# Differential attention: two banks' low-part score products on 64-row halves of the array, and VectorE's scaling put between the two maxima

## The reference, cut to what matters

```python
s = einsum('bqhmd,bkhmd->bhmqk', q, k) * QK_DIM ** -0.5     # m = 0, 1: two maps for each head
p = softmax(s, axis=-1)
a = p[:, :, 0] - lam * p[:, :, 1]
o = einsum('bhqk,bkhd->bqhd', a, v)
```

## Time and profile before

| what | us |
| --- | --- |
| median of 3 runs (lowest to highest) | 1229.45 (1229.1 to 1230.09) |
| the profiled execution: its time; its span in the trace | 1230.16; 1228.4 |
| TensorE's matmuls busy (share of the span) | 1104.3 (90%) |
| VectorE busy | 608.9 (50%) |
| ScalarE busy | 415.6 (34%) |
| GpSimd busy | 238.0 (19%) |
| attention stage, from its first matmul to the last scaling | 480.9 to 681.9 |

### The profile page before, as it was taken

The page is one execution under the profiler, slowest core; times in us unless marked ns, Lnnn a source line. Parts: engine busy times, 40 slices in busy tenths (PEclk is TensorE's granted clock), DMA queues, the critical chain, the costliest instruction groups (busy, mean ns, idle before and its releaser), DMA issues. The chain is left out here.

```text
span 1228.4 us, 20703 instructions
## 1 busy us (share of the span) xinstructions
PE 1104.3 (90%) x7006; PEld 794.9 (65%) x7006; DVE 608.9 (50%) x1049; ACT 415.6 (34%) x831; POOL 238.0 (19%) x163
## 2 busy tenths in 40 slices
PE   5799999998999997989889799997899869899965
PEld 1687777777999886888788688887533213233332
DVE  0763545204564687767777456666133222233336
ACT  2651111113423774666566546631000000000012
POOL 0000000003000394457666100000111010010041
PEclk9899999999999998899999899998799989999988
DMA  9436677622100544460611333313968873768266
GB/s 362 143 127 235 231 236 237 192 69 79 42 21 1 126 115 132 79 142 24 153 35 52 109 135 106 118 70 134 376 225 279 267 269 124 267 226 264 114 241 255
DMA packets 127944, 196.96 MB, mean 160 GB/s; under 512 B 20592, under 2 KB 93200, under 8 KB 125790
## 3 DMA queue, kind: packets, MB, share of 16 engines
q1 hardware_dynamic: 98700, 144.39, 36.7%
q10 hardware_dynamic: 23378, 30.27, 7.1%
q0 software_dynamic: 5760, 20.97, 5.2%
HBM read 382.85 MB, written 39.24 MB: 344 GB/s over the span
## 5 line engine op out<-in xcount | busy, mean ns | idle before, releaser
L2199 PE MATMUL experts_gu_ps<-moe_wgu,experts_xT 128*32 128x512 f32 x1408 | 169.2, 620 | 18.7 <-DMA moe_wgu<-in_w_exp_up 18.1
L103 PE MATMUL proj_acc_ps<-proj_w_hi,hidden_hT_hi 128*128 128x512 f32 x288 | 117.5, 408 | 6.7 <-DVE hidden_hT_lo L98 6.7
L2199 PEld LDWEIGHTS experts_gu_ps<-moe_wgu,experts_xT 128*32 128x32 f32 x1408 | 43.9, 112 | 121.7 <-issue 101.9
L105 PE MATMUL proj_acc_ps<-proj_w_hi,hidden_hT_lo 128*128 128x512 f32 x288 | 114.8, 399 | 0.0
L104 PE MATMUL proj_acc_ps<-proj_w_lo,hidden_hT_hi 128*128 128x512 f32 x288 | 114.3, 397 | 0.0
L1334 POOL TENSOR_TENSOR att_e<-att_e 128x1152 f32<-128x1152 f32 (+1 forms) x36 | 86.1, 2392 | 71.2 <-DVE att_e L1415 71.2
L1352 ACT ACTIVATE att_e<-att_sc_ps,att_shift 128x1152 f32<-128x1152 f32 (+1 forms) x72 | 81.5, 1132 | 40.2 <-DVE att_shift L1404 39.9
L2220 PE MATMUL experts_y_ps<-moe_wd,experts_hidT 128*32 128x512 f32 x704 | 81.6, 605 | 9.3 <-issue 8.0
L1404 DVE TENSOR_REDUCE att_shift<-att_sc_ps 128x1 f32<-128x1152 f32 (+1 forms) x72 | 86.2, 1231 | 6.7 <-PE att_sc_ps L1449 6.6
L1478 PE MATMUL att_turned_ps<-att_in_v_tok,att_aT 128*128 128x128 f32 x584 | 77.2, 280 | 8.3 <-ACT att_aT L1360 8.1
L2169 POOL DMA_INDIRECT experts_xg<-scratch_h,all_step_token x22 | 30.9, 1406 | 257.0 <-PE experts_x_ps L2184 231.5
(11 more groups left out here) (380 smaller groups left out, 2158.1 us busy)
## 6 DMA issues: line engine op xcount, KB each, us to landing
moe_wgu<-in_w_exp_up ACTq DMA_DIRECT2D x356, 256.0 KB
moe_wgu<-in_w_exp_gate SPq DMA_DIRECT2D x356, 256.0 KB
moe_wd<-in_w_exp_down SPq DMA_DIRECT2D x89, 1024.0 KB
scratch_y_slots<-experts_y ACTq DMA_DIRECT2D x22, 512.0 KB, 5.5
proj_raw<-in_w_in SPq DMA_DIRECT2D x32, 256.0 KB, 5.0
proj_feat<-in_w_ada SPq DMA_DIRECT2D x4, 2048.0 KB, 8.4
proj_xh<-in_w_ada SPq DMA_DIRECT2D x4, 2048.0 KB, 9.9
proj_feat<-in_w_ada SPq DMA_DIRECT2D x4, 1024.0 KB, 8.0
```

What stands on the lines that cost most here:

```text
L103: pe.matmul(out, a_high, b_high, start=start, stop=False)
L105: return pe.matmul(out, a_low, b_high, start=False, stop=stop)
L2199: mm = pe.matmul(gu_ps[n % 2][at, :], xT[:, n % 2, k * P + c * Q:k * P + (c + 1) * Q], wgu[:, c, k], start=(k == 0), stop=(k == KT - 1))
```

## The change

First, the low-part products. `scores` now issues the three high-key matmuls of a map one after another, and then three matmuls that use only 64 of the array's rows: query high times key low, without low times low. Two of them stand on opposite halves of the rows and write different banks, the third is on the first one's half again. For this each half of the rows holds other banks' low keys, and the high part of the query stands on both halves (in a third slab). Second, VectorE's `maximum(k, 0)` moves ahead of `scale_second(k-1)`. Third, `load_stack` issues 18 loads in place of 12.

```diff
+SCORES = TILES * P // 3
+STACK_LOADS = 18
 def load_stack(sp, W, h):
+    keys, queries, done = W["keys"][h % 2], W["queries"][h % 2], W["stack_in"][h % 2]
     for m in range(2):
         rows = slice(m * QKD, (m + 1) * QKD)
-        for part, src in enumerate((W["k_high"], W["k_low"])):
-            for half in range(2):
-                sp.dma_start(W["keys"][h % 2][half * QKD:(half + 1) * QKD, m, part].bitcast(F32), src[h, rows, :]
-                             ).then_inc(W["stack_in"][h % 2], 16)
-        for half, src in enumerate((W["q_high"], W["q_low"])):
-            sp.dma_start(W["queries"][h % 2][half * QKD:(half + 1) * QKD, m].bitcast(F32), src[h, rows, :]
-                         ).then_inc(W["stack_in"][h % 2], 16)
+        own, other = (slice((m ^ half) * QKD, ((m ^ half) + 1) * QKD) for half in range(2))
+        banks = [slice(P + b * SCORES, P + (b + 1) * SCORES) for b in range(3)]
+        for half in (own, other):
+            sp.dma_start(keys[half, m].bitcast(F32), W["k_high"][h, rows, :]).then_inc(done, 16)
+        low = W["k_low"][h, rows, :]
+        for half, to, src in ((own, slice(0, P), slice(0, P)), (own, banks[0], banks[m]), (own, banks[1], banks[2]),
+                              (other, banks[2], banks[1 - m])):
+            sp.dma_start(keys[half, 2, to].bitcast(F32), low[:, src]).then_inc(done, 16)
+        for half, slab, src in ((own, m, "q_high"), (other, m, "q_low"), (other, 2, "q_high")):
+            sp.dma_start(queries[half, slab].bitcast(F32), W[src][h, rows, :]).then_inc(done, 16)
...
                 if k >= 3:
                     finish(items[k - 3])
+                if k < N:
+                    maximum(items[k], 0)
                 if 1 <= k <= N:
                     scale_second(items[k - 1])
                 if k < N:
-                    maximum(items[k], 0)
                     maximum(items[k], 1)
...
-                q = queries[it.stack][:, m, it.t * P:(it.t + 1) * P]
-                for b in range(1 if it.prompt else 3):
-                    width = P if it.prompt else BANK
-                    cols = slice(it.first_key + b * BANK, it.first_key + b * BANK + width)
-                    out = sc[m][:, b * 512:b * 512 + width]
-                    pe.matmul(out, q, keys[it.stack][:, m, 0, cols], start=True, stop=False)
-                    mm = pe.matmul(out, q, keys[it.stack][:, m, 1, cols], start=False, stop=True)
-                mm.then_inc(sc_done[m], 1)
+                q, k = (stack[it.stack] for stack in (queries, keys))
+                at, own, other = slice(it.t * P, (it.t + 1) * P), slice(m * QKD, (m + 1) * QKD), slice((1 - m) * QKD, (2 - m) * QKD)
+                if it.prompt:
+                    out = sc[m][:, 0:P]
+                    pe.matmul(out, q[:, m, at], k[:, m, 0:P], start=True, stop=False)
+                    pe.matmul(out, q[own, m, at], k[own, 2, 0:P], start=False, stop=True).then_inc(sc_done[m], 1)
+                    return
+                banks = [sc[m][:, b * 512:b * 512 + BANK] for b in range(3)]
+                cols = [slice(P + b * BANK, P + (b + 1) * BANK) for b in range(3)]
+                for b in range(3):
+                    pe.matmul(banks[b], q[:, m, at], k[:, m, cols[b]], start=True, stop=False)
+                pe.matmul(banks[m], q[own, m, at], k[own, 2, cols[0]], start=False, stop=True)
+                pe.matmul(banks[1 - m], q[other, 2, at], k[other, 2, cols[2]], start=False, stop=True)
+                pe.matmul(banks[2], q[own, m, at], k[own, 2, cols[1]], start=False, stop=True).then_inc(sc_done[m], 1)
```

12 lines of the change are left out of this document (6 added, 6 removed).

## The result

The changed kernel is slower. Four runs on the first chip gave 1235.59, 1238.89, 1239.85 and 2199.03 us; the last lies far outside and is left out, so the median is 1238.89. The ratio to the kernel before, 1229.28 beside these runs, is 1.0065 (95% interval 1.0034 to 1.0097). The forecast was 1226.0, its range 1219 to 1233.

The account below looks back on a forecast made before the run. A 5.58 us ring of scaling, first maximum and two exponentials was taken to bound full items; -1.4 - 0.3 - 1.0 - 1.2 + 0.2 = -3.7 us gave 1225.8 on the median, stated as 1226.0, own range 1223.5 to 1229, wider range 1219 to 1233.

Parts of the forecast that it names:

- The ring: Full items: ring of scaling, first maximum, exponentials (5.58 us) gives way to one over GpSimd's sum, 5.49, with 64-row matmuls 5.53.
- The 64-row group: Scores' matmuls on TensorE: overlap saves a 0.17 us slot, passages cost more; scores end 0.04 earlier, what follows starts 0.13 later.
- rival of free passages: Scores' 64-row matmuls: passages cost nothing, each group saves 0.17 us, ring 5.32, total -9.6, 1219.8 us; chance 0.2.
- that of turns: Scores' 64-row matmuls: halves take turns, group keeps all slots and pays passages; ring 5.71, total +1.3, 1230.8 us; chance 0.2.
- rival of the paid halves: Scores' 64-row matmuls: each change of half paid like a mode change; TensorE 6.56 us per item, +27 us, 1254; chance 0.1.
- The steady term: Steady full items of the attention stage: 28 items at 5.53 in place of 5.58 us, -1.4 us.
- Start of the stage: Second full item: its maximum no longer waits behind the scaling, so TensorE's next transposes start earlier, -1.0 us.
- Three more are at the heads' second full items: Scores waiting behind an exponential there: it comes over 1 us earlier, GpSimd's sum takes most back; -0.4 each, -1.2 us.
- The head changes: Steps over the short item between heads: the forecast's sum has no term for them.
- the end: End of the attention stage: the last scaling comes 0.2 later, +0.2 us.
- L98: GpSimd's split step beside VectorE's scaling, eight times: delay 0.36 each in place of 0.29, later rings partly absorb it; -0.3 us.
- GpSimd or the clock: Rival: late weights for GpSimd cost time, or two more slow-clock stretches at 1.2 GHz add 4.8 us, 1231; chance 0.1.

Follow-up runs that it names:

- the thirds: GpSimd's output-weight split cut by columns into three equal steps: on the changed kernel 1237.68 us (1.0061), on the kernel before with VectorE's new order 1230.64 us (1.0005).
- the second look: The kernel before, unchanged, profiled once more: 1230.07 us, clock 0.958.
- the second batch: Later timing of the changed kernel, unchanged, twelve more runs: median 1235.36 us, ratio 1.0044 to the kernel before, clock 0.9501 against 0.9547.
- the 64-row matmuls alone: The changed kernel with VectorE's old order restored, keeping the 64-row matmuls and 18 loads: 1235.23 us, ratio 1.0028 to the kernel before, clock 0.9457.
- the second profile of the changed kernel: Profile from running the changed kernel again, unchanged, beside the other kernels; its timed runs had a median of 1235.36 us, ratio 1.0044.
- order alone: The kernel before with only VectorE's first maximum moved ahead of the scaling: 1232.01 us, ratio 1.0016.

## Why the prediction failed

*The ring.* Right in kind. 5.58 us was the ring over the scaling, the new one over GpSimd's sum gives 5.50 with the 64-row group (forecast 5.53) and 5.41 without it (forecast 5.49), and the waits have the releasers that were named.

*The 64-row group.* Right within 0.02 us: passage 0.27, halves together, third matmul at 0.55 (0.46 to 0.53 forecast), scores' end at 0.89 (0.80 to 0.87), next instruction at 0.82 (0.81 to 0.88). The rival of free passages and that of turns are out. The third load, on the half of the first matmul, did not wait for it: it starts at 525.96, 0.11 behind that matmul's start. The Trainium skill, *TensorE: Matmul & The Clock Gate*, The mechanism, has a load pulled ahead when its row group does not conflict or when it goes to the background weight buffer; the row group is the same here, so by that page it would be the buffer, which the trace does not show. (In the rival of the paid halves, 5.88 us an item should have given 1235.5 and not 1234; nothing hangs on it.)

*The steady term: -1.4.* Right in kind and a little small: in the steady run an item takes 5.50 us in place of 5.58, so 28 items win an estimated 2.2.

*Start of the stage: -1.0.* Right: from the first maximum of item 1 to that of item 3 it is 10.12 us, before 11.12; the next interval, at the low clock in both, gives 0.25 back (7.70 against 7.45).

*"Three more are at the heads' second full items": -0.4 each.* Right where it was meant. TensorE's wait behind the exponential of a head's second full item was 2.43, 2.45 and 2.20 us before and is 1.13 or 1.14 after (timelines, before and after, the first of the three):

```profile
544.70 0.69 PE L1448 MATMUL att_sc_ps<-att_keys,att_queries 128*128 128x384 f32 x1 [2.43 <-ACT att_e L1352]
```

```profile
545.51 0.79 PE L1462 MATMUL att_sc_ps<-att_keys,att_queries 128*128 128x384 f32 x3 [1.13 <-ACT att_e L1360]
```

The sum takes a part back. In the third head, at full clock in both, it is 5.13 us from the second full item's scores to the third's and 6.26 on to the fourth's (together 11.39); after, 4.19 and 6.79 (10.98): -0.4.

*The head changes: no term.* This step failed. The sum counts 28 steady items, the stage's start, the heads' second full items and the end; the step over the short item was put at nothing, without a reason. I did not walk the new ring through it. GpSimd's sum is that of a full item there, so what the short scores had saved in the old order is lost: 0.94, 0.98 and 0.98 us, +2.9 in all. That takes back nearly all that the full items win: at full clock the nine items from 17 to 26 take 50.83 us before and 50.68 after.

*L98.* -0.3 forecast, from 0.36 us for each of eight. The scalings' excess grew by 5.2 us instead (9.1 against 3.9), since the scaling met the subtraction near its start. In the row the term was mis-sized; what it is worth in the time is not shown, since the thirds have a price of their own.

*The clock.* The rival "GpSimd or the clock" at 0.1 had the price right in kind ("two more such stretches make +4.8") and no reason why there should be more. Its other half did not come: GpSimd waited 9.0 us for weights before and 3.8 after. What the runs show: passages in every group go with a lower granted clock in the first head (0.82 against 0.90), and the mean over whole runs is lower. The price can be read from the two profiles of the changed kernel, where one of them has 3.4 us more at 1.2 GHz in a head: cut at the scores, its seven full items take 1.08, 0.95 and 1.03 us longer (40.20 against 39.12, 40.88 against 39.93, 41.88 against 40.85), 0.3 us for each us at 1.2 GHz. From its first matmul to its last scaling the stage takes 3.5 us more than before in the first profile, with 7.9 us more at 1.2 GHz, and 4.8 more in the second against the second look, with 13.6. So the clock is an estimated 2.4 and 4.1 us of these, and about 1 us is left at equal clock. The forecast, -3.7, with the +2.9 of the head changes is -0.8; the 1.5 to 2 us between them are not attributed here, and L98 is a candidate.

In whole runs, within one kernel, a run with a clock lower by 0.01 is longer by 5.0 us (slope common to 16 kernels with 272 timed runs, standard error 0.5). By that slope the change's 0.0046 in the second batch is 2.3 us of its 5.4 us of mean difference; by 0.3 us for each us at 1.2 GHz it is an estimated 3.4. The 0.009 of the 64-row matmuls alone is 4.5 of 5.0 by the slope.

*What stays open.* Two to 3 of the 5.4 us are not located for certain. What lies behind the stage does not help: from the first maximum of item 35 to the end it is 554.1 us after, 552.1 and 551.5 before, but 551.3 in the second profile of the changed kernel, where the attention stage alone accounts for all of the 3.3 us by which its span is longer than that of the second look (1231.6 against 1228.3). And why passages go with a low clock is shown only as far as the experiments above tell.

## What to carry to other kernels

When a change replaces the ring that sets the period, walk the new ring through every irregular step as well: an item that is short for one engine shortens the step only if it is short for every engine on the ring. Price a few 64-row matmuls among 128-row ones with their passages, here 0.28 us there and back, so that an overlapped pair of 384 columns (0.17 us) does not pay for one passage. Cut the windows of before and after at an event that the change does not itself move: here a maximum that the new order brought forward by 1 us doubled both the gain and the loss. And look at the granted clock before believing a span: here it is 2.3 to 3.4 of 5.4 us.

## What the runs showed of the hardware

One unexpected thing: the kernels with the busier TensorE had the lower clock. Its stretch with 39.93 of 41.50 us busy was granted 0.82, the one with 36.29 of 40.90 busy 0.90, and 44.50 of 45.49 got 0.78. The low clock makes a part of the busy share itself, since matmuls last longer in it (eight transposes 1.91 us in the earlier trace rows, 1.03 in the earlier trace rows). The Trainium skill, *TensorE: Matmul & The Clock Gate*, Part 1 (the HAM clock gate), has the clock rise with activity and fall in idle stretches; a busy share as the profile counts it does not order these rows.

Also, GpSimd's and VectorE's exclusion was nearly complete (2.47 us for a 0.82-us instruction, 0.62 of it behind GpSimd's end), and a kernel with five such scalings (order alone, 8.7 us over 0.82 in all) was level with the kernel before.
